# Cross-attention with its operands split into high and low parts, on one core

## The reference, cut to what matters

```python
def memory_cross_attention(h, mem_n, wq, wkv, wo):
    Bsz, L, _ = h.shape
    M = mem_n.shape[1]
    q = (h @ wq).reshape(Bsz, L, XA_HEADS, XA_HEAD_DIM)
    k, v = jnp.split(mem_n @ wkv, 2, axis=-1)
    k = k.reshape(Bsz, M, XA_HEADS, XA_HEAD_DIM)
    v = v.reshape(Bsz, M, XA_HEADS, XA_HEAD_DIM)
    s = jnp.einsum('blhd,bmhd->bhlm', q, k).astype(jnp.float32) * (XA_HEAD_DIM ** -0.5)
    p = jax.nn.softmax(s, axis=-1)
    o = jnp.einsum('bhlm,bmhd->blhd', p.astype(v.dtype), v).reshape(Bsz, L, XA_WIDTH)
    return o @ wo
```

## Time and profile before

| | us |
|---|---|
| three runs | 1341.08, 1342.60, 1350.21 |
| median of the runs | 1342.6 |
| the profiled execution's own time | 1340.88 |
| its span | 1339.1 |
| PE busy | 1323.8 |
| DVE busy | 738.4 |
| ACT busy | 340.8 |
| POOL busy | 320.2 |

### The profile page before, as it was taken

How to read it: one execution, slowest core, us unless ns; L and a number is a source line. 1 busy time by engine, 2 the same in 40 slices (tenths; PEclk the granted TensorE clock), 3 DMA queues, 4 the chain that set the end, 5 groups by cost and what they waited for, 6 DMA issues and landing times.

```text
span 1339.1 us, 17122 instructions
## 1 busy us (share of the span) xinstructions
PE 1323.8 (99%) x6354; PEld 1083.3 (81%) x6354; DVE 738.4 (55%) x1066; ACT 340.8 (25%) x703; POOL 320.2 (24%) x358
## 2 busy tenths in 40 slices
PE   9999999999999999999999999999999999999998
PEld 7887678888788888888888878888788888888886
DVE  7886856447584443234444778567674443334432
ACT  3338255212331110001111347423321110001122
POOL 2222234311322111112111126413211111221110
PEclk9999999999999999999999999999999999999999
DMA  6333222232333333333323332132333332333322
GB/s 224 103 110 95 79 80 80 79 94 95 110 94 94 95 95 104 100 95 94 94 95 112 103 110 69 52 94 94 95 94 94 96 106 97 95 94 94 95 94 94
DMA packets 97664, 130.36 MB, mean 97 GB/s; under 512 B 6304, under 2 KB 62880, under 8 KB 97600
## 3 DMA queue, kind: packets, MB, share of 16 engines
q1 hardware_dynamic: 95728, 127.16, 30.2%
q10 hardware_dynamic: 1872, 2.31, 0.6%
HBM read 124.67 MB, written 2.10 MB: 95 GB/s over the span
## 4 chain that ended last, share of the span: by engine, by line
PE 92%; DVE 4%; issue 1%; DMA 1%; POOL 1%; ACT 0%; DVEq 0%; POOLq 0%; ACTq 0%
PE ps L617 26%; PE ps L621 26%; PE ps L620 26%; PE ps L1150 1%; PE ps L1153 1%; PE ps L1154 1%; PE ps L982 1%; PE ps L745 1%; PE ps L998 1%; PE ps L720 1%; PE ps L1011 1%; DVE xc L1441 1%; DVE w_lo L1182 1%; DMA raw<-in_w_in 1%; PE ps L816 1%
## 5 line engine op out<-in xcount | busy, mean ns | idle before, releaser
L1182 DVE TENSOR_TENSOR w_lo<-raw,w_hi 128x1024 fp32r<-128x1024 f32 x226 | 279.4, 1237 | 420.8 <-POOL w_hi L548 419.6
L548 POOL TENSOR_SCALAR w_hi<-raw 128x1024 fp32r<-128x1024 f32 x226 | 248.4, 1099 | 922.2 <-DMA raw<-in_w_gate_up 404.5
L617 PE MATMUL ps<-z_hi,w_hi 128*128 128x512 f32 x1040 | 409.9, 394 | 1.9 <-ACTq L1896 1.8
L621 PE MATMUL ps<-z_hi,w_lo 128*128 128x512 f32 x1040 | 405.8, 390 | 0.0
L620 PE MATMUL ps<-z_lo,w_hi 128*128 128x512 f32 x1040 | 405.7, 390 | 0.0
L617 PEld LDWEIGHTS ps<-z_hi,w_hi 128*128 128x128 f32 x1040 | 195.9, 188 | 50.0 <-issue 5.6
L620 PEld LDWEIGHTS ps<-z_lo,w_hi 128*128 128x128 f32 x1040 | 195.9, 188 | 41.6 <-issue 1.4
L621 PEld LDWEIGHTS ps<-z_hi,w_lo 128*128 128x128 f32 x1040 | 195.8, 188 | 41.1
L617 PE MATMUL ps<-f_hi,w_hi 128*128 128x512 f32 x528 | 208.0, 394 | 0.8 <-DVEq L1518 0.8
L621 PE MATMUL ps<-f_hi,w_lo 128*128 128x512 f32 x528 | 205.6, 389 | 0.0
L620 PE MATMUL ps<-f_lo,w_hi 128*128 128x512 f32 x528 | 205.5, 389 | 0.0
(11 more groups left out here) (201 smaller groups left out, 1254.1 us busy)
## 6 DMA issues: line engine op xcount, KB each, us to landing
raw<-in_w_gate_up SPq DMA_DIRECT2D x176, 256.0 KB
raw<-in_w_down SPq DMA_DIRECT2D x44, 512.0 KB
raw<-in_w_in SPq DMA_DIRECT2D x20, 512.0 KB
raw<-in_w_out SPq DMA_DIRECT2D x20, 512.0 KB
raw<-in_xa_wkv SPq DMA_DIRECT2D x16, 512.0 KB
raw<-in_w_in SPq DMA_DIRECT2D x16, 256.0 KB
raw<-in_xa_wq SPq DMA_DIRECT2D x8, 512.0 KB
raw<-in_xa_wo SPq DMA_DIRECT2D x8, 512.0 KB
```

Of the source, the lines that this page charges most:

```text
L548: pool.tensor_scalar(w_hi[:, slot], raw[:, slot], 1.0, 1.0, ALU.mult, ALU.mult).then_inc(s_hi, 1)
L617: ins = pe.matmul(o, whi, rhi, start=start, stop=False)
L621: return pe.matmul(o, wlo, rhi, start=False, stop=stop)
L1182: dve.tensor_tensor(w_lo[:, slot], raw[:, slot], w_hi[:, slot].bitcast(F32), ALU.subtract).then_inc(s_lo, 1)
```

## The change

Queries, keys, values and the turned probabilities are each held as a rounded high part and a rounded low part, and the products of the scores and of the values become three products of such tiles. Keys are split once a layer after `one_over_rms` (ACT high, DVE low), each query tile after it has been scaled, the values after `values_scaled`. The turned probabilities are no longer copied: ACT writes the high part of both banks, DVE the low part of both. `mk_lo`, `mv_lo` and `qx_lo` overwrite `mk`, `mv` and `qx`. `values_scaled` is split in two, and `fill(3)` too: its first half (the value bank 0) now stands ahead of `turns(1)`, its second half behind it. `turns(3)` moves ahead of `values(1)`. In the DVE and ACT programs the steps are put in a new order. The tile `gain` of the final norm moves by 8192 bytes. The core of the diff:

```diff
@@ PE, attention
                 def scores(n):
-                    ready(n)
+                    if n == 0:
+                        pe.wait_ge(s_xl, 8 * l + 2)
+                    pe.wait_ge(s_xl, 8 * l + 2 + n + 1)
                     if n >= 2:
                         pe.wait_ge(a["s_read"], n - 1)
                     b0 = BANK * (a["bank"](0) + 2 * (n % 2))
                     for i, k0_, nk, c in a["scores"]:
-                        ins = pe.matmul(flat[:, b0 + c:b0 + c + nk], q(n)[:, i * P:(i + 1) * P],
-                                        key(n)[:, k0_:k0_ + nk], start=True, stop=True)
+                        o = flat[:, b0 + c:b0 + c + nk]
+                        qh, ql = qx_hi[:, n, i * P:(i + 1) * P], qx_lo[:, n, i * P:(i + 1) * P]
+                        kh, kl = mk_hi[:, n, k0_:k0_ + nk], mk_lo[:, n, k0_:k0_ + nk]
+                        ins = pe.matmul(o, qh, kh, start=True, stop=False)
                         if n == 0 and i == 0:
                             ins.then_inc(s_used, 1)
+                        pe.matmul(o, qh, kl, start=False, stop=False)
+                        ins = pe.matmul(o, ql, kh, start=False, stop=True)
                     ins.then_inc(a["s_scores"], 1)
...
                 def values(n):
                     pe.wait_ge(a["s_pt"], 2 * (n + 1))
-                    if n == 0:
-                        pe.wait_ge(a["s_filled"], 2)
...
-                        ins = pe.matmul(ps[:, a["o_banks"][n % 2], q0_:q0_ + nq], value(n, j),
-                                        a["prob_t"][n % 3][:, src:src + nq], start=start, stop=x_ == last)
+                        if n == 0:
+                            pe.wait_ge(s_xl, 8 * l + 6 + j + 1)
+                        o, c = ps[:, a["o_banks"][n % 2], q0_:q0_ + nq], slice(P * n, P * (n + 1))
+                        th, tl = a["prob_th"][n % 3][:, src:src + nq], a["prob_tl"][n % 3][:, src:src + nq]
+                        pe.matmul(o, mv_hi[:, j, c], th, start=start, stop=False)
+                        pe.matmul(o, mv_hi[:, j, c], tl, start=False, stop=False)
+                        ins = pe.matmul(o, mv_lo[:, j, c], th, start=False, stop=x_ == last)
...
                 fill(2)
+                fill(3, (0,))
                 turns(1)
-                fill(3)
+                fill(3, (1,))
                 turns(2)
                 values(0)
+                turns(3)
                 values(1)
-                turns(3)
                 values(2)
@@ DVE
+            def keys_low(l):
+
+                for b in range(2):
+                    dve.wait_ge(s_xh, 8 * l + b + 1)
+                    dve.tensor_tensor(mk_lo[:, 2 * b:2 * b + 2, :], mk[:, 2 * b:2 * b + 2, :],
+                                      mk_hi[:, 2 * b:2 * b + 2, :].bitcast(F32), ALU.subtract).then_inc(s_xl, 1)
...
+            def query_low(l, t):
+
+                dve.wait_ge(s_xh, 8 * l + 2 + t + 1)
+                dve.tensor_tensor(qx_lo[:, t, :], qx[:, t, :], qx_hi[:, t, :].bitcast(F32), ALU.subtract).then_inc(s_xl, 1)
...
                 def turned(n):
-                    dve.wait_ge(a["s_turned"], n + 1)
                     if n >= 3:
                         dve.wait_ge(a["s_head"], n - 2)
-                    t0 = a["bank"](4) * BANK
-                    dve.tensor_copy(a["prob_t"][n % 3][:, BANK:], flat[:, t0 + BANK:t0 + 2 * BANK]).then_inc(a["s_pt"], 1)
+                    for half in range(2):
+                        dve.wait_ge(s_pth, 2 * XH * l + 2 * n + half + 1)
+                        c, t0 = slice(BANK * half, BANK * (half + 1)), (a["bank"](4) + half) * BANK
+                        dve.tensor_tensor(a["prob_tl"][n % 3][:, c], flat[:, t0:t0 + BANK],
+                                          a["prob_th"][n % 3][:, c].bitcast(F32), ALU.subtract).then_inc(a["s_pt"], 1)
 
                 maxima(0)
+                query_low(l, 3)
                 maxima(1)
                 low_to(u0 + 3)
                 denominator(0)
...
                 low_to(u0 + 5)
+                values_scaled(a, 0)
                 turned(1)
+                values_low(l, 0)
                 denominator(3)
-                values_scaled(a)
+                values_scaled(a, 1)
+                values_low(l, 1)
                 turned(2)
+                output(a, 0, 0)
                 low_to(u0 + 6)
-                output(a, 0, 0)
+                turned(3)
                 output(a, 1, 1)
-                turned(3)
...
                 one_over_rms(f"xa{l}")
+                keys_low(l)
                 for t in range(4):
                     scaled(qx[:, t, :], GROUP0[f"xq{l}"], t, s_done[f"xq{l}"], t + 1)
                     dve.nop().then_inc(s_xq, 1)
-                attention(ATTN[f"xattn{l}"])
+                    if t:
+                        query_low(l, t - 1)
+                attention(ATTN[f"xattn{l}"], l)
@@ ACT, attention
-                    t0 = a["bank"](4) * BANK
-                    act.activation(a["prob_t"][n % 3][:, 0:BANK], flat[:, t0:t0 + BANK], ACT.Copy).then_inc(a["s_pt"], 1)
-
+                    for half in range(2):
+                        t0 = (a["bank"](4) + half) * BANK
+                        act.activation(a["prob_th"][n % 3][:, BANK * half:BANK * (half + 1)], flat[:, t0:t0 + BANK],
+                                       ACT.Copy).then_inc(s_pth, 1)
+
+                def values_high(t):
+                    act.wait_ge(a["s_filled"], t + 1)
+                    act.activation(mv_hi[:, t, :], mv[:, t, :], ACT.Copy).then_inc(s_xh, 1)
+
+                act.wait_ge((mx, wn)[l]["s_filled"], XH)
+                for b in range(2):
+                    act.activation(mk_hi[:, 2 * b:2 * b + 2, :].rearrange("p a n -> p (a n)"),
+                                   mk[:, 2 * b:2 * b + 2, :].rearrange("p a n -> p (a n)"), ACT.Copy).then_inc(s_xh, 1)
+                for t in range(4):
+                    act.wait_ge(s_xq, XH * l + t + 1)
+                    act.activation(qx_hi[:, t, :], qx[:, t, :], ACT.Copy).then_inc(s_xh, 1)
                 exps(0)
                 exps(1)
                 exps(2)
                 turned(0)
                 exps(3)
                 act.nop().then_inc(s_free[GROUP0[a["name"]] % 2], 4)
+                values_high(0)
                 turned(1)
+                values_high(1)
                 turned(2)
                 output(a, 0, 0)
+                turned(3)
                 output(a, 1, 1)
-                turned(3)
```

More of the change, by code:

```diff
@@ L192, in trunk @@
         qx = at("qx", [P, 4, T], F32, z_q)
+        qx_hi, qx_lo = at("qx_hi", [P, 4, T], F32R, z_v), at("qx_lo", [P, 4, T], F32R, z_q)
+        mk_hi, mk_lo = at("mk_hi", [P, XH, M], F32R, z_k), at("mk_lo", [P, XH, M], F32R, z_mk)
+        mv_hi, mv_lo = at("mv_hi", [P, MB, 512], F32R, z_k + 4096), at("mv_lo", [P, MB, 512], F32R, z_mv)
         xpad = [at(f"xpad{i}", [P, T + CONV], F32, z_k + 2080 * i) for i in range(2)]
@@ L211, in trunk @@
         y_in = at("y_in", [P, 2, T], F32, z_mv)
-        gain = at("gain", [P, D], F32, z_x)
+        gain = at("gain", [P, D], F32, z_x + 8192)
         row_sq = at("row_sq", [P, 2 * TB, BANK], F32, z_zh)
@@ L301, in trunk @@
             z_turned = z_zh + 12 * a["width"]
-            a["prob_t"] = [at(f"prob_t_{name}{i}", [P, a["t_width"]], F32, z_turned + 4 * a["t_width"] * i) for i in range(3)]
-            assert z_turned + 12 * a["t_width"] <= z_raw
+            homes = [z_turned, z_turned + 8 * a["t_width"], z_x]
+            a["prob_th"] = [at(f"prob_th_{name}{i}", [P, a["t_width"]], F32R, o) for i, o in enumerate(homes)]
+            a["prob_tl"] = [at(f"prob_tl_{name}{i}", [P, a["t_width"]], F32R, o + 4 * a["t_width"]) for i, o in enumerate(homes)]
+            assert z_turned + 16 * a["t_width"] <= z_raw
             for s in ("scores", "max", "read", "exp", "rden", "prob", "turned", "pt", "head", "o_hi", "o_lo",
@@ L706, in z_ready, with attention @@
                 return lambda k: pe.wait_ge(s_zl, NORM[norm] * DB + k + 1)
-            def attention(a, q, key, value, ready, fill, next_unit):
+            def attention(a, l, fill, next_unit):
                 g = GROUP0[a["name"]]
@@ L799, in memory_keys, with memory_values @@
                             ins.then_inc(a["s_filler"], 1)
-            def memory_values(l, j):
+            def memory_values(l, j, tiles=range(MB)):
                 a, u0 = ATTN[f"xattn{l}"], UNIT0[f"xattn{l}"]
@@ L806, in memory_values @@
                 half = (u0 + j) % SLOTS
-                for t in range(MB):
+                for t in tiles:
                     o = ps[:, a["o_banks"][t], :]
@@ L1114, in _ @@
                 xo = (f"xo{l}", 2, f, s_done[f"xo{l}"], lambda k: pe.wait_ge(ax["s_o_lo"], k + 1))
-                attention(ax, lambda n: qx[:, n, :], lambda n: mk[:, n, :],
-                          lambda n, j: mv[:, j, P * n:P * (n + 1)], lambda n: pe.wait_ge(s_xq, XH * l + n + 1),
-                          lambda j: memory_values(l, j), ahead(*xo))
```

(3 more changed lines are left out.)

15 lines of the change are left out of this document (9 added, 6 removed).

## The result

Over 20 runs each the kernel after takes 1351.87 us and the kernel before 1342.45: a ratio of 1.0066 [1.0054, 1.0078], 8.9 us more (7.2 to 10.5). (The medians are 9.4 apart; the 8.9 goes by the ratio.) The forecast was 1351.2.

A forecast was written before the change was run, and what follows sets the result against it. PE was taken as the bound, busy 1323.8 of 1339.1 us. Per layer 6.5 idle + 0.2 restarts - 2.8 saved + 0.4 meetings gave +4.3, or +8.6 for two: 1351.2 us, range 1341.5 to 1358.

The forecast's parts named there:

- PE's products: Scores and values of the cross-attention: three rounded products cheaper than one f32 product, saving 2.8 us a layer, 5.6 in all.
- The start: Before scores 0: DVE makes low keys and tile 0's low part first, leaving PE 1.84 us idle.
- Scores 2: Before scores 2: PE waits for head 0's exponentials, delayed by DVE's later maxima; 0.7 us idle.
- The table load: Exponential's table on ACT, loaded behind the last query copy: takes 1.28 us, hidden by 0.15, no drain counted.
- Turns 2 and values 0: PE waits for low parts: 2.3 us idle before turns 2, 1.2 before the second value bank, 0.4 before turns 3.
- The hand-over to PE: Passing a semaphore to PE, wherever PE waits for a feeder: put at 0.1 us, bounds 0 and 0.3 a place.
- The sum: Per layer 6.5 us idle plus 0.2 restarts less 2.8, with 0.4 for meetings: +4.3, +8.6 for two layers.
- the term for meetings: DVE's eight added subtractions a layer may be slowed beside POOL: 0 to 1.2 us, taken as 0.4.
- B: Rival: the clock falls at the gap around turns 2, once a layer, 1.8 us a fall; 1354.8 us; chance 0.25.
- C: Rival: smaller stalls in the attention through more overlap; 1337.0 us if all idle went, 1344.7 if half; chance 0.18.
- D: Rival: the clock falls at the first gap too, both places of both layers, four times 1.8 us; 1358.4; chance 0.10.
- E: Rival: three rounded products no cheaper than one f32 product in the attention, 5.6 us come back; 1356.8; chance 0.05.

The follow-up runs named there:

- first_gap: Kernel after with keys split ahead of the reciprocal and the low parts of queries 2 and 3 made later; 1350.87 us, ratio 1.0069 [1.0045, 1.0093].
- pool_later: Kernel after with POOL's split of the last unit of the values moved behind the normalising of head 0; 1346.39 us in a single run.
- scores_only: Kernel after with only queries and keys split, values and turned probabilities back in f32 form and order; 1346.7 us, ratio 1.0038 [1.002, 1.0055].
- products_only: Kernel before with each f32 product of scores and values made three times from one rounded tile, no low parts; 1336.67 us, ratio 0.9958 [0.994, 0.9977].

## Why the prediction was right

The walk through the feeders can be laid over the trace, step by step. Times are from the end of `xq`, in us (329.2 in the prediction, 333.96 in layer 0 of after, 928.22 in layer 1):

| step | predicted | layer 0 | layer 1 |
|---|---|---|---|
| scores 0 begin | 1.8 | 1.91 | 1.81 |
| scores 2 begin | 8.25 | 8.33 | 9.10 |
| turns 2 begin | 23.5 | 23.33 | 24.09 |
| second value product | 26.25 | 25.95 | 26.72 |
| turns 3 begin | 27.45 | 27.24 | 28.01 |
| last values end | 37.9 | 37.73 | 38.46 |

**PE's products.** 2.8 us a layer were predicted and 2.6 measured alone. The scores came 0.12 apart and the values 0.23, as read from the earlier trace rows and from the fills. The missing 0.2 about fits the first value product behind each group of transposes, 0.31 instead of 0.23.

**The start.** Predicted 1.84 of idle. From turn to turn it is 1.91 and 1.81. The releaser is `query_low` of tile 0 in both layers, the chain that the step named.

**Scores 2.** Predicted 0.7; layer 0 has 0.70 from turn to turn. Layer 1 has 1.56, and the surplus is the small row of DVE that POOL held up. The sum had 0.4 us a layer for a meeting of the two, between 0 and 1.2; it came as 0 in layer 0 and 0.86 in layer 1, 0.43 a layer. That the mean fits is luck, since one layer had none and the other twice as much; and the carrier was another: I had put it on the eight new subtractions, and it fell on a row of 128x4 that was there before.

The table load stands where it was foretold. ACT in the kernel after, ahead of the exponentials of layer 0:

```profile
338.05 0.63 ACT L1889 ACTIVATE qx_hi<-qx 128x512 fp32r<-128x512 f32 x1 [0.90 <-DVEq L1712]
338.70 1.28 ACT L1864 ACT_TABLE_LOAD   x1
340.17 0.47 ACT L1864 ACTIVATE prob_xattn<-ps,stat 128x256 f32<-128x256 f32 x1 [0.19 <-DVE stat L1335]
```

It ends at 339.98, 0.19 before the exponentials' own input does, so it is hidden by 0.19 (0.15 predicted). The drain of about 1380 ns that the Trainium skill counts with each load ("ScalarE: Activation LUTs", section "What ACT_TABLE_LOAD costs") does not appear: with it the exponentials could not have begun at 340.17.

**Turns 2 and values 0.** Predicted 2.3, 1.2 and 0.4 of idle; from turn to turn 2.08, 1.02 and 0.47 in layer 0, and 2.06, 1.03 and 0.48 in layer 1. POOL ended the high part of `u0 + 5` at 352.75, 18.8 after the start, where the walk had 18.95; the rest of the chain, low part, value scaling, ACT's copies, DVE's low parts, ran in the order and with the prices of the walk. Two gaps came out 0.2 smaller. At turns 2 most of that is POOL's unit, ready 0.15 sooner than in the walk, and the steps behind it kept the lead. The hand-over to PE, put at 0.1 a place, was 0.15, 0.14 and 0.05 from the end of DVE's row to PE's at the first scores, turns 2 and values 0.

**The sum.** The gaps add to 6.2 and 6.9, less 2.6 for the products: 3.6 and 4.3, beside 3.7 and 4.4 measured by the stretch; the last 0.1 is PE's restarts, for which 0.2 stood in the sum. Predicted 4.3 a layer, measured 4.06 on average. The walk was right in its steps, but that the forecast of 1351.2 lies within 0.7 us of the median is partly luck: the idle was 0.3 too large in layer 0, the saving 0.2 too large, the term for meetings fell on one layer alone, and two of the three base runs were 1.5 and 7.6 us off the median. The timed difference itself is known to 1.6 us only.

**The rivals.** B (the clock falls at turns 2) did not happen in the profiled execution of the kernel after: the granted clock is 1.00 through both attentions. Of the other 19 only the mean clock is known, 0.992 to 0.998 and once 0.945 (at 1353.75 us), so they can't rule out a fall now and then. It did happen in layer 0 of `first_gap` and of `pool_later`, where that gap is 2.71 and 2.48. C (smaller stalls) is refuted by the gaps. D had a real mechanism, seen once in `scores_only`, at a price of 0.8 us of stretch and not 1.8. E is refuted by `products_only` and by the products' distances in the kernel after. One thing was wrong in B and D alike, the price of 1.8 us for a fall: layer against layer the three falls slowed PE's products by 1.1 to 1.3 us, and what of this reached the stretch was 0.8 in `scores_only` and 0.1 each in `first_gap` and `pool_later`, because the rest filled waits that PE had in the other layer.

## What to carry to other kernels

In a kernel whose PE is busy 99% of the time, cheaper products are a gain only as long as their operands come in time. Here they were worth 5.2 us, and the order of the feeders' work decided whether this was seen: the same computation came out at +8.1 and at -4.3 us. A new operand should be made ahead of whatever PE needs later, in every feeder's program, and each step of preparation be walked through to the instruction of PE that waits; mending the first gap alone moved part of the wait to the next one. To judge a few microseconds in a kernel whose executions spread by ten, compare a stretch bounded by the same two instructions in each trace.

## What the runs showed of the hardware that was not expected

**A tiny DVE instruction can be held for a whole POOL instruction.** 0.17 us became 1.05 for 128x4 numbers where POOL had begun 0.02 us ahead; where DVE had begun 0.01 ahead it stayed at 0.17, and the next subtraction took 1.54. Moving the meeting moved the cost.

**The same idle, two outcomes for the clock.** The windows of `first_gap` behind the gap of 2.71 us in layer 0, and behind the one of 2.70 in layer 1:

```profile
354.00:356.00 2.00, 1.74 (x10) 1.68 (x11) 1.44 (x4) 0.53 (x1) 1.11 (x3) 0.73 0.22 27
356.00:358.00 2.00, 2.00 (x6) 0.99 (x4) 1.87 (x3) 1.07 (x3) 2.00 (x3) 0.50 0.85 296
...
948.00:950.00 2.00, 1.14 (x8) 0.66 (x6) 1.30 (x3) 1.43 (x3) 2.00 (x4) 1.00 0.51 151
950.00:952.00 2.00, 1.67 (x10) 1.22 (x11) 1.51 (x3) 0.77 (x2) 2.00 (x3) 1.00 0.93 357
```

In layer 0 the clock went to 1.2 GHz for some 3 us, in layer 1 it stayed at 2.4, and both stretches are 36.53. The slow products of layer 0 took 1.3 us more, and 1.2 of it filled the time that PE in layer 1 spent waiting (0.86 and 0.33) for the next low parts; the last 0.1 is hidden in the stretch by a first gap that was 0.1 shorter in layer 0. A fall costs only what it takes beyond the waits behind it. `pool_later` shows the pair again (2.48 with a fall, 2.49 without, 0.1 of the stretch), `scores_only` at 1.77 and 1.71 (0.8). What decides between them these runs don't show.

**The gates' gap** of 2.8 to 3.0 us at 97 to 99 us is there in four profiles of twelve, always together with the idle at 78 to 80, and in both profiles of one and the same kernel; whether it belongs to the kernel's layout or to the execution is open.
